# Hybrid block kernel, one core: GpSimd held back at the feed-forward boundaries, squares added on VectorE, and the experts' down projection as three split products

## The chip, the cores and the metric

The kernel runs on one core of a Trainium2 chip. The metric is the device time of one execution in microseconds (us), as the median of several executions. The kernel before took 2161.84 us (median of 3, 2158.42 to 2165.49).

The engines are TensorE (PE in the profile, its weight loads PEld), VectorE (DVE), ScalarE (ACT), GpSimd (POOL) and SyncE (SP), which only issues transfers here. Each runs its own list of instructions in order and waits on semaphores.

## What is computed

Two transformer-like blocks run after each other on 512 tokens of width 1024, in float32. The parts that matter here are the mixture of experts that ends the first block, the two feed-forward layers of the second, and the norms around them. The reference, cut to these:

```python
def hier_moe(h, ...):
    ...
    for gi in range(N_GROUPS):              # 4 groups of 4 experts
        hg = jnp.einsum('td,edf->etf', hf, w_exp_gate[sl])
        hu = jnp.einsum('td,edf->etf', hf, w_exp_up[sl])
        act = jax.nn.silu(hg) * hu * combine[:, sl].T[:, :, None]
        y = y + jnp.einsum('etf,efd->td', act, w_exp_down[sl]).astype(hf.dtype)
...
def swiglu(x, w_in, w_out):
    a, b = jnp.split(x @ w_in, 2, axis=-1)
    return (jax.nn.silu(a) * b) @ w_out
...
    h = h + 0.5 * rms_norm_2(swiglu(rms_norm_2(h, g_ffn1_pre), w_ffn1_in, w_ffn1_out), g_ffn1_post)
    u = rms_norm_2(h, g_mix_pre)
    ...
    h = h + rms_norm_2(mixed, g_mix_post)
    h = h + 0.5 * rms_norm_2(swiglu(rms_norm_2(h, g_ffn2_pre), w_ffn2_in, w_ffn2_out), g_ffn2_post)
```

## The kernel before

**Split products.** Nearly every product is made of three: a float32 operand x is split into hi (x rounded to the fp32r type, a copy on ACT) and lo (x minus hi, a subtraction on DVE or POOL), and PE adds hi*hi, hi*lo and lo*hi in PSUM. In the dense stages ACT makes `w_hi`, POOL makes `w_lo` (`split_chunk`, L722 to L728) from a ring of three weight chunks `w_raw`.

**The experts.** Tokens are sorted by group, so that 7 blocks of 128 rows meet 4 experts each: 28 units (`UNITS`). A unit has three 1 MB chunks of weights: A and B (the two halves of gate and up) and C (down). They lie in 6 slots (`M_SLOTS`), and SP loads a chunk into a slot when PE has used up the chunk six places earlier (semaphore `m_used`), which for A, B and C is two units back. PE's order in its loop over u is: gate_up_half(u+1, A), transpose_act(u), gate_up_half(u+1, B), down(u). ACT copies the hi parts of A and B (L2030, 128x2048 each), DVE subtracts the lo parts (`expert_lo`, L2867). After a unit's gate and up, ACT makes the silu (`silu_of`, L2087), DVE multiplies (`weigh`, L3019, tile `m_act`), PE transposes (L1382) and ACT copies the transposed rows to `m_aT` (`act_rows`, L2093). The down product `down(u)` (L1395) is native float32: 4 matmuls of 512 columns straight from `m_raw` and `m_aT`; the profile shows each as two MATMUL rows. In iteration n ACT's order is hi A(n+2), hi B(n+2), act_rows(n), silu(n+1); DVE's is lo A(n+2), lo B(n+2), weigh(n+1). POOL has nothing in this stage.

**The feed-forward layers.** `swiglu` runs 11 units. A unit has two "seven" chunks (gate, up), computed as seven block products in place of eight (`seven_products`), for which DVE forms sums of weight blocks (`weight_sums`, L2328 to L2332), ACT copies `w_hi` and `wx_hi`, and POOL subtracts `w_lo` (L727) and `wx_lo` (L738, `split_seven`). DVE adds up the seven results (`block_sums`) before PE can use the four PSUM slots again. On entry DVE also splits the normed input by blocks (`h_blocks`, L2300 and L2304). The unit's down product accumulates into `yacc` (L3129).

**The norms.** The sum of squares over the 8 tiles of the feature axis needs all of them: ACT squares each tile (L1647), PE sums the first `own` tiles by products with a column of ones (L905), and DVE adds tiles own+1 to 7 to tile own (`add_square`, L2338), which PE sums last. `SQ_DENSE = 2` is own in the norms next to dense products, `SQ_PACED = 5` in the norm that follows another norm. `keep_clock` (L892) issues products of the identity with itself, whose result nobody reads.

## Time and profile before

| what | value |
|---|---|
| median of 3 runs | 2161.84 us |
| the profiled execution | 2168.82 us, its span 2166.8 us |
| PE busy | 2078.1 us (96%) |
| DVE busy | 1279.4 us (59%) |
| ACT busy | 833.1 us (38%) |
| POOL busy | 788.1 us (36%) |
| moved from HBM | 257.6 MB |
| stages, from the span's start: experts / first feed-forward / second | 654 to 923 / 964 to 1331 / 1797 to 2151 us |

All times in what follows are us from the start of the span. The profile puts a busy PE at 96% of the span; since matmul ends are modelled, this doesn't say that PE computes at its peak for so long. The profiled execution took 7.0 us more than the median of the others.

### The profile page before, as it was taken

The page shows a single profiled execution, that of the slowest core. Times are in us where ns is not written, and L with a number is a line of the kernel's source. Part 1 is how long each engine was busy: PE and PEld are TensorE (multiplying, and loading weights), DVE is VectorE, ACT ScalarE, POOL GpSimd, SP SyncE. Part 2 cuts the span into 40 slices and gives each one's busy share as a digit, 9 for nine tenths or more (in the row PEclk, how much of TensorE's full clock was granted, in tenths as well). Part 3 has the DMA queues.
Part 4 walks back from the last instruction along what each step waited for, and adds up shares of the span by engine and source line. Part 5 has one row for each costly group of instructions (what it writes and reads, how often), then busy time and mean ns, then how long its engine had stood idle before and what let it go on. Part 6 is the DMA issues. An engine that isn't in the chain of part 4 may idle for free.

```text
span 2166.8 us, 31293 instructions
## 1 busy us (share of the span) xinstructions
PE 2078.1 (96%) x12492; PEld 1777.2 (82%) x12492; DVE 1279.4 (59%) x1959; ACT 833.1 (38%) x1018; POOL 788.1 (36%) x595
## 2 busy tenths in 40 slices
PE   4999999999999999979999999999999998999998
PEld 4698787888767666669999999888878788999997
DVE  7375476555465656477677676332431358777775
ACT  7441255222345555344333333343332234333332
POOL 1341233444300000036556552221244435656660
PEclk7898999999989999979999998999999999999999
DMA  9122213555317999712322221111123212223321
GB/s 266 39 79 72 85 59 98 188 191 171 110 59 262 337 342 344 248 59 89 107 97 97 97 97 39 59 59 59 59 78 98 78 59 78 98 97 106 107 97 59
DMA packets 175760, 261.12 MB, mean 121 GB/s; under 512 B 12233, under 2 KB 140922, under 8 KB 175662
## 3 DMA queue, kind: packets, MB, share of 16 engines
q1 hardware_dynamic: 174126, 257.65, 35.8%
q10 hardware_dynamic: 1536, 2.10, 0.3%
q8 instruction: 69, 1.13, 0.2%
q14 instruction: 29, 0.24, 0.0%
HBM read 257.62 MB, written 2.11 MB: 120 GB/s over the span
## 4 chain that ended last, share of the span: by engine, by line
PE 86%; DVE 7%; ACT 4%; issue 1%; POOL 1%; DMA 1%; SPq 0%; DVEq 0%; POOLq 0%; ACTq 0%
PE PS L798 64%; PE PS L1355 7%; PE PS L1395 5%; PE PS L1524 1%; DVE Hf L2368 1%; ACT mod_early L1725 1%; PE PS L892 1%; PE PS L885 1%; DVE Hf L2338 1%; POOL w_lo L727 1%; PE PS L1328 1%; PE PS L1476 1%; DMA mod_early<-in_w_mod 1%; PE PS L905 1%; PE PS L1036 0%
## 5 line engine op out<-in xcount | busy, mean ns | idle before, releaser
L727 POOL TENSOR_TENSOR w_lo<-w_raw,w_hi 128x512 fp32r<-128x512 f32 x444 | 595.5, 1372 | 1287.0 <-ACT w_hi L1703 1265.0
L798 PE MATMUL PS<-HH,w_hi 128*128 128x512 f32 (+2 forms) x1408 | 471.3, 346 | 23.7 <-DVE HL L2291 7.9
L798 PE MATMUL PS<-HL,w_hi 128*128 128x512 f32 (+2 forms) x1408 | 467.3, 343 | 0.0
L798 PE MATMUL PS<-HH,w_lo 128*128 128x512 f32 (+2 forms) x1408 | 465.7, 342 | 0.0
L1703 ACT ACTIVATE w_hi<-w_raw 128x2048 fp32r<-128x2048 f32 x133 | 254.8, 1916 | 392.0 <-DVE w_raw L2329 147.9
L798 PEld LDWEIGHTS PS<-HH,w_hi 128*128 128x128 f32 x1408 | 264.0, 192 | 61.7 <-issue 21.3
L798 PEld LDWEIGHTS PS<-HH,w_lo 128*128 128x128 f32 x1408 | 263.9, 192 | 30.8
L798 PEld LDWEIGHTS PS<-HL,w_hi 128*128 128x128 f32 x1408 | 263.5, 192 | 30.0
L738 POOL TENSOR_TENSOR wx_lo<-wx_raw,wx_hi 128x512 fp32r<-128x512 f32 x132 | 190.0, 1467 | 6.5 <-DVE Hf L2338 6.5
L2867 DVE TENSOR_TENSOR m_lo<-m_raw,m_hi 128x2048 fp32r<-128x2048 f32 x56 | 128.5, 2297 | 76.8 <-ACT m_hi L2030 76.6
L3129 DVE TENSOR_TENSOR yacc<-yacc,PS 128x528 f32<-128x528 f32 (+1 forms) x176 | 117.8, 691 | 49.4 <-PE PS L798 48.6
L798 PE MATMUL PS<-ah,w_hi 128*128 128x264 f32 (+1 forms) x528 | 142.6, 324 | 2.6 <-DVE al L3122 2.6
L2030 ACT ACTIVATE m_hi<-m_raw 128x2048 fp32r<-128x2048 f32 x56 | 107.2, 1916 | 91.9 <-DMA m_raw<-in_w_exp_up 91.9
L798 PE MATMUL PS<-al,w_hi 128*128 128x264 f32 (+1 forms) x528 | 141.5, 322 | 0.0
L798 PE MATMUL PS<-ah,w_lo 128*128 128x264 f32 (+1 forms) x528 | 141.5, 322 | 0.0
L798 PE MATMUL PS<-HHx,wx_hi 128*128 128x264 f32 (+1 forms) x352 | 100.2, 285 | 3.5 <-DVE HLx L2300 2.4
L1395 PE MATMUL PS<-m_raw,m_aT 128*128 128x512 f32 x224 | 101.3, 595 | 1.4 <-ACT m_aT L2093 1.2
L798 PE MATMUL PS<-HHx,wx_lo 128*128 128x264 f32 (+1 forms) x352 | 100.1, 284 | 0.0
L798 PE MATMUL PS<-HLx,wx_hi 128*128 128x264 f32 (+1 forms) x352 | 100.0, 284 | 0.0
L798 PEld LDWEIGHTS PS<-ah,w_hi 128*128 128x128 f32 x528 | 88.5, 190 | 10.5 <-DVE al L3122 3.3
L798 PEld LDWEIGHTS PS<-ah,w_lo 128*128 128x128 f32 x528 | 88.2, 190 | 7.7
L798 PEld LDWEIGHTS PS<-al,w_hi 128*128 128x128 f32 x528 | 88.2, 190 | 7.0
(498 smaller groups left out, 4087.1 us busy)
## 6 DMA issues: line engine op xcount, KB each, us to landing
w_raw<-in_w_in SPq DMA_DIRECT2D x49, 1024.0 KB, 5.1
w_raw<-in_w_ffn_in SPq DMA_DIRECT2D x44, 1024.0 KB, 4.8
m_raw<-in_w_exp_gate SPq DMA_DIRECT2D x56, 512.0 KB, 4.3
m_raw<-in_w_exp_up SPq DMA_DIRECT2D x56, 512.0 KB, 5.4
m_raw<-in_w_exp_down SPq DMA_DIRECT2D x56, 512.0 KB, 4.8
w_raw<-in_w_ffn_out SPq DMA_DIRECT2D x22, 1024.0 KB, 4.8
mod_late<-in_w_mod SPq DMA_DIRECT2D x16, 1024.0 KB, 5.2
mod_early<-in_w_mod SPq DMA_DIRECT2D x8, 1024.0 KB, 11.9
```

The costliest lines, as they stand in the source:

```text
L727: ins = pool.tensor_tensor(w_lo[:, s, cs], w_raw[:, s, cs], w_hi[:, s, cs].bitcast(F32), ALU.subtract)
L738: ins = pool.tensor_tensor(wx_lo[s][:, q], wx_raw[s][:, q], wx_hi[s][:, q].bitcast(F32), ALU.subtract)
L798: ins = mm(o, l, r, **k)
L885: ins = mm(PS[:, s, bank, col:col + G], rsc[0:G, c0 + j:c0 + j + 1].to_broadcast([G, P]), ident[0:G, 0:G], start=True, stop=True)
L892: mm(PS[:, s, 1, 0:P], ident[:, :], ident[:, :], start=True, stop=True)
L905: ins = mm(PS[0:G, s, 0, j:j + 1], Hf[:, k, G * j:G * j + G], ones[:, 0:1], start=k == 0 and j == 0, stop=k == own, skip_group_check=True)
L1355: ins = mm(PS[:, 0, expert_bank(u), :].rearrange("p (g f) -> p g f", g=2), l[:, kk, :], r[:, :, k, :], start=kk == 0 and n == 0, stop=kk = ...
L1395: ins = mm(PS[:, 2 + blk % 2, b, :], m_aT[:, k, :], w[:, k, 512 * b:512 * b + 512], start=ee == 0 and k == 0, stop=ee == N_GRP - 1 and k == 1)
L1703: af(w_hi[:, c % RING, :], w_raw[:, c % RING, :], ACT.Copy).then_inc(hi_done, 1)
L2030: af(m_hi[x][:, :], m_raw[x][:, :], ACT.Copy).then_inc(m_hi_done, 1)
L2867: tt(m_lo[x][:, :], m_raw[x][:, :], m_hi[x][:, :].bitcast(F32), ALU.subtract).then_inc(m_lo_dve, 1)
L3129: W.release(tt(y, y, ps(s, T), ALU.add))
```

## The change

It has four parts.

1. **Down projection.** The transposed activations are split in two (`m_aTH` on ACT, `m_aTL` on DVE), and so is chunk C (`down_hi` on ACT, `down_lo_of` on DVE, 128x2048 each). `down(u)` is 12 products of 512 columns in place of 4 native ones, and waits for `d_lo_done` and `atl_ready`.
2. **Squares.** `SQ_DENSE` becomes 0: in the dense norms DVE adds tiles 1 to 7 to tile 0 and PE sums only that one. The norm before the first feed-forward keeps 2 (`SQ_UNSORT`). PE issues 8 `keep_clock` products before it waits for the sum (`hold`).
3. **POOL.** It waits for the squares' sum before it splits the first chunk of the first feed-forward (before: only between the chunk and its extra blocks), and for the four block sums of the input before the second chunk's extra blocks; and it waits for the sums of the two norms behind the first feed-forward before chunks 1 and 3 of the mixer.
4. **Order.** In `swiglu` the weight sums of the fourth chunk are made before the block sums of the second product and not after them. At the end PE transposes the first half of two tokens' tiles rather than of four before the sum of squares.

```diff
 D = 1024
-SQ_DENSE = 2
+SQ_DENSE = 0
+SQ_UNSORT = 2
 SQ_PACED = 5
...
 m_act = ar("m_act", 33792, [2, P])
-m_aT = ar("m_aT", 34816, [2, P])
+m_aTH = ar("m_aTH", 34816, [2, P], F32R)
+m_aTL = ar("m_aTL", 35840, [2, P], F32R)
 YSH = hf("YSH", KT * TALL * 4, [NTOK, D], F32R)
...
 t_made = sem("expert_act_transposed")
-at_ready = sem("expert_act_rows_ready")
+at_ready = sem("expert_act_rows_hi_ready")
+atl_ready = sem("expert_act_rows_lo_ready")
+d_hi_done = sem("expert_down_hi")
+d_lo_done = sem("expert_down_lo")
 y_added = sem("block_y_added")
...
-    def split_seven(c, s, more=0, sums=None):
+    def split_seven(c, s, more=0, blocks=None):
...
         split_chunk(c, s, more)
-        if sums is not None:
-            pool.wait_ge(sqsum_ready, sums)
+        if blocks is not None:
+            pool.wait_ge(t_ready, blocks)
         pool.wait_ge(hix_done, seven_made(c) + 1 + more * 2)
...
         c = FF_AT[n]
-        split_seven(c, c % RING, sums=2 if n == 0 else None)
+        if n == 0:
+            pool.wait_ge(sqsum_ready, 2)
+        split_seven(c, c % RING)
         if n == 1:
             pool.wait_ge(sqsum_ready, 6)
-        split_seven(c + 1, (c + 1) % RING)
+        split_seven(c + 1, (c + 1) % RING, blocks=4 if n == 0 else None)
         with pool.Fori(0, FF_UNITS - 1) as i:
...
     mixer_at = FF_AT[0] + n_ff
-    rounds = (FF_AT[1] - mixer_at) // RING
+    pool.wait_ge(sqsum_ready, 3)
+    for c in range(mixer_at, mixer_at + RING):
+        if c == mixer_at + 2:
+            pool.wait_ge(sqsum_ready, 4)
+        split_chunk(c, c % RING)
+    rounds = (FF_AT[1] - mixer_at) // RING - 1
     with pool.Fori(0, rounds) as i:
         for s in range(RING):
-            split_chunk(mixer_at + s, (mixer_at + s) % RING, i)
-    for c in range(mixer_at + RING * rounds, FF_AT[1]):
+            split_chunk(mixer_at + RING + s, (mixer_at + s) % RING, i)
+    for c in range(mixer_at + RING * (rounds + 1), FF_AT[1]):
         split_chunk(c, c % RING)
...
-    def sum_squares(T, own):
+    def sum_squares(T, own, hold):
...
             if k == own:
+                keep_clock(hold, s)
                 hcount["sum"] += 1
...
-    def norm(T, own, idle):
-
-        s = sum_squares(T, own)
+    def norm(T, own, hold, idle):
+
+        s = sum_squares(T, own, hold)
         keep_clock(3, s)
...
-    norm(SEQ, SQ_DENSE, 5)
+    norm(SEQ, SQ_DENSE, 8, 5)
...
             pe.wait_ge(at_ready, u - 1)
+            pe.wait_ge(atl_ready, u - 1)
         for k in range(2):
...
         blk, ee = u // N_GRP, u % N_GRP
-        pe.wait_ge(m_landed[x], 32 * (chunk_c(u) // M_SLOTS + 1))
-        pe.wait_ge(at_ready, u + 1)
+        pe.wait_ge(d_lo_done, u + 1)
+        pe.wait_ge(atl_ready, u + 1)
         if ee == 0 and blk >= 2:
             pe.wait_ge(y_added, blk - 1)
-        w = m_raw[x][:, :].rearrange("p (k n) -> p k n", k=2)
+        hi = m_hi[x][:, :].rearrange("p (k n) -> p k n", k=2)
+        lo = m_lo[x][:, :].rearrange("p (k n) -> p k n", k=2)
         for k in range(2):
-            for b in range(2):
-                ins = mm(PS[:, 2 + blk % 2, b, :], m_aT[:, k, :], w[:, k, 512 * b:512 * b + 512],
-                         start=ee == 0 and k == 0, stop=ee == N_GRP - 1 and k == 1)
+            for n, (l, r) in enumerate(((m_aTH, hi), (m_aTH, lo), (m_aTL, hi))):
+                for b in range(2):
+                    ins = mm(PS[:, 2 + blk % 2, b, :], l[:, k, :], r[:, k, 512 * b:512 * b + 512],
+                             start=ee == 0 and k == 0 and n == 0, stop=ee == N_GRP - 1 and k == 1 and n == 2)
         ins.then_inc(m_used, 1)
...
-    norm(TALL, SQ_DENSE, 20)
+    norm(TALL, SQ_UNSORT, 8, 20)
     swiglu(FF_UNITS, TALL)
-    norm(TALL, SQ_DENSE, 28)
-    norm(TALL, SQ_PACED, 20)
+    norm(TALL, SQ_DENSE, 8, 28)
+    norm(TALL, SQ_PACED, 0, 20)
     await_h(now=False)
...
     out_projection()
-    norm(SEQ, SQ_DENSE, 28)
-    norm(SEQ, SQ_PACED, 20)
+    norm(SEQ, SQ_DENSE, 8, 28)
+    norm(SEQ, SQ_PACED, 0, 20)
+
...
     s = W.claim()
-    for k in range(SQ_DENSE):
-        pe.wait_ge(sq_ready, hcount["sq"] + k + 1)
-        for j in range(NTOK):
-            mm(PS[:, s, 0, j:j + 1], Hf[:, k, P * j:P * j + P], ones[:, 0:1], start=k == 0 and j == 0, stop=False,
-               skip_group_check=True)
     pe.wait_ge(gain_diag_ready, 1)
     pe.wait_ge(rtok_ready, 2 * NTOK)
-    for k in range(4):
-        W.wait_released(downs_at + k)
-        for t in range(NTOK):
+    for t in range(2):
+        for k in range(4):
+            W.wait_released(downs_at + k)
             rows_of_y((s + 1 + t) % SLOTS, t, k)
...
     for j in range(NTOK):
-        ins = mm(PS[:, s, 0, j:j + 1], Hf[:, SQ_DENSE, P * j:P * j + P], ones[:, 0:1], start=False, stop=True,
+        ins = mm(PS[:, s, 0, j:j + 1], Hf[:, SQ_DENSE, P * j:P * j + P], ones[:, 0:1], start=j == 0, stop=True,
                  skip_group_check=True)
...
         slot = W.claim()
-        for k in range(4, KT):
+        for k in range(4 if t < 2 else 0, KT):
             if t == 0:
...
             act.wait_ge(m_used, chunk_c(u - 1) + 1)
-        af(m_aT[:, :, :].rearrange("p k n -> p (k n)"), PS[:, 1, u % 2, 0:256], ACT.Copy).then_inc(at_ready, 1)
+        af(m_aTH[:, :, :].rearrange("p k n -> p (k n)"), PS[:, 1, u % 2, 0:256], ACT.Copy).then_inc(at_ready, 1)
+
+    def down_hi(u):
+        x = chunk_c(u) % M_SLOTS
+        act.wait_ge(m_landed[x], 32 * (chunk_c(u) // M_SLOTS + 1))
+        af(m_hi[x][:, :], m_raw[x][:, :], ACT.Copy).then_inc(d_hi_done, 1)
     silu_of(0)
+    down_hi(0)
     block_hi(1)
...
             silu_of(n + 1)
+            down_hi(n + 1)
         if n % N_GRP == 1 and n > N_GRP and n // N_GRP + 1 < BLOCKS:
...
+    def act_rows_lo(u):
+        dve.wait_ge(at_ready, u + 1)
+        tt(m_aTL[:, :, :].rearrange("p k n -> p (k n)"), PS[:, 1, u % 2, 0:256],
+           m_aTH[:, :, :].rearrange("p k n -> p (k n)").bitcast(F32), ALU.subtract).then_inc(atl_ready, 1)
+
+    def down_lo_of(u):
+        x = chunk_c(u) % M_SLOTS
+        dve.wait_ge(d_hi_done, u + 1)
+        tt(m_lo[x][:, :], m_raw[x][:, :], m_hi[x][:, :].bitcast(F32), ALU.subtract).then_inc(d_lo_done, 1)
+
     def add_block(blk):
...
     weigh(0)
+    down_lo_of(0)
     block_lo(1)
...
             expert_lo(2 * n + 5)
+        act_rows_lo(n)
         if n + 1 < UNITS:
             weigh(n + 1)
+            down_lo_of(n + 1)
         if n % N_GRP == 1 and n > N_GRP and n // N_GRP + 1 < BLOCKS:
...
             weight_sums(FF_AT[0] + 1)
-        if m > SQ_DENSE + 1:
-            add_square(Hf, TALL, m - 1, SQ_DENSE)
+        if m > SQ_UNSORT + 1:
+            add_square(Hf, TALL, m - 1, SQ_UNSORT)
     for b in range(1, 5):
...
         weight_sums(at_ + 2)
+        weight_sums(at_ + 3)
         block_sums(actf)
-        weight_sums(at_ + 3)
         gated(0, 0)
...
     real = lambda k: R[:, k, META:TALL]
-    norm(TALL, every, c2(0), SQ_DENSE, split="blocks", while_summed=lambda: clear_y(TALL, 0, 4),
+    norm(TALL, every, c2(0), SQ_UNSORT, split="blocks", while_summed=lambda: clear_y(TALL, 0, 4),
          while_spread=lambda: clear_y(TALL, 4, KT))
...
             weight_sums(FF_AT[1] + 1)
-        if m > SQ_DENSE + 1:
+        if m == 4:
+            for k in range(SQ_DENSE + 1, 4):
+                add_square(Hf, SEQ, k, SQ_DENSE)
+        if m > 4:
             add_square(Hf, SEQ, m - 1, SQ_DENSE)
```

What stands in DVE's list for one unit of the experts in the middle of the stage, before:

```order
L3019 ISA [waits expert_silu_ready]
L3019 SCALAR_TENSOR_TENSOR m_act<-PS,wtab,m_sg 128x128x2
L2867 TENSOR_TENSOR m_lo_222<-m_raw_221,m_hi_223 128x2048 [waits expert_chunk_hi]
L2867 TENSOR_TENSOR m_lo_225<-m_raw_224,m_hi_226 128x2048 [waits expert_chunk_hi]
L3019 ISA [waits expert_silu_ready]
```

and with the change:

```order
L3050 TENSOR_TENSOR m_lo_220<-m_raw_219,m_hi_221 128x2048 [waits expert_down_hi]
L2886 TENSOR_TENSOR m_lo_223<-m_raw_222,m_hi_224 128x2048 [waits expert_chunk_hi]
L2886 TENSOR_TENSOR m_lo_226<-m_raw_225,m_hi_227 128x2048 [waits expert_chunk_hi]
L3044 TENSOR_TENSOR m_aTL<-PS,m_aTH 128x256 [waits expert_act_rows_hi_ready]
L3038 ISA [waits expert_silu_ready]
```

The row of `m_aTL`, for which down(n) waits on PE, stands behind the lo parts of both chunks of unit n+2. ACT's list for the same stretch, before and with the change:

```order
L2030 ACTIVATE m_hi_223<-m_raw_221 128x2048 [waits expert_chunk_landed2]
L2030 ACTIVATE m_hi_226<-m_raw_224 128x2048 [waits expert_chunk_landed3]
L2093 ACTIVATE m_aT<-PS 128x256 [waits expert_chunk_used,expert_act_transposed]
L2087 ACTIVATE m_sg<-PS 128x256 [waits expert_chunk_used,expert_act_ready]
L2030 ACTIVATE m_hi_232<-m_raw_230 128x2048 [waits expert_chunk_landed5]
```

The same stretch of ACT with the change:

```order
L2042 ACTIVATE m_hi_233<-m_raw_231 128x2048 [waits expert_chunk_landed5]
L2042 ACTIVATE m_hi_218<-m_raw_216 128x2048 [waits expert_chunk_landed0]
L2105 ACTIVATE m_aTH<-PS 128x256 [waits expert_chunk_used,expert_act_transposed]
L2099 ACTIVATE m_sg<-PS 128x256 [waits expert_chunk_used,expert_act_ready]
L2110 ACTIVATE m_hi_221<-m_raw_219 128x2048 [waits expert_chunk_landed1]
```

A third copy, that of chunk C, has come in behind each silu. On POOL, at the entry of the first feed-forward, before:

```order
L727 TENSOR_TENSOR w_lo_50<-w_raw_49,w_hi_51 128x512 [waits chunk_hi_done,chunk_extra_blocks_ready]
L727 TENSOR_TENSOR w_lo_50<-w_raw_49,w_hi_51 128x512 x3
L738 TENSOR_TENSOR wx_lo0_180<-wx_raw0_179,wx_hi0_181 128x512 [waits chunk_extra_hi_done,squares_of_last_tiles_added]
...
L727 TENSOR_TENSOR w_lo_50<-w_raw_49,w_hi_51 128x512 [waits chunk_hi_done,chunk_extra_blocks_ready]
...
L738 TENSOR_TENSOR wx_lo1_183<-wx_raw1_182,wx_hi1_184 128x512 [waits chunk_extra_hi_done]
```

and with the change:

```order
L732 TENSOR_TENSOR w_lo_50<-w_raw_49,w_hi_51 128x512 [waits chunk_hi_done,chunk_extra_blocks_ready,squares_of_last_tiles_added]
L732 TENSOR_TENSOR w_lo_50<-w_raw_49,w_hi_51 128x512 x3
L743 TENSOR_TENSOR wx_lo0_180<-wx_raw0_179,wx_hi0_181 128x512 [waits chunk_extra_hi_done]
...
L732 TENSOR_TENSOR w_lo_50<-w_raw_49,w_hi_51 128x512 [waits chunk_hi_done,chunk_extra_blocks_ready]
...
L743 TENSOR_TENSOR wx_lo1_183<-wx_raw1_182,wx_hi1_184 128x512 [waits chunk_extra_hi_done,h_block_sums_ready]
```

The wait for the squares has moved ahead of the first chunk, and the second chunk's extra blocks have a new one.

## Rows read from the trace of the kernel before

**Rows 1.** Windows of 40 us: busy time and (count) by engine, PE clock, DMA share, GB/s.

```profile
760.00:800.00 40.00, 40.00 (x152) 27.33 (x151) 23.88 (x15) 20.92 (x18) 0.00 (x0) 1.00 0.96 341
```

**Rows 2.** Instructions by line, 700 to 880: count, busy us, mean ns, idle before and releaser.

```profile
L2867 DVE TENSOR_TENSOR m_lo<-m_raw,m_hi 128x2048 fp32r<-128x2048 f32 x39 | 89.4, 2293 | 57.3 <-ACT m_hi L2030 57.3
L2030 ACT ACTIVATE m_hi<-m_raw 128x2048 fp32r<-128x2048 f32 x38 | 72.9, 1917 | 65.7 <-DMA m_raw<-in_w_exp_up 65.7
```

**Rows 3.** Chain of waits, 640 to 960: start, us, engine and line.

```profile
673.07 3.43 PE PS L1395 x8
...
839.67 3.43 PE PS L1395 x8
846.08 2.77 PE PS L1355 x12
848.85 3.43 PE PS L1395 x8
```

**Rows 4.** Timeline of SP, 820 to 860: start, us, line, operation.

```profile
839.84 0.33 SPq L648 DMA_DIRECT2D m_raw<-in_w_exp_gate  x1
```

**Rows 5.** Timeline of ACT, 820 to 850, the same columns, idle before in brackets.

```profile
846.14 1.92 ACT L2030 ACTIVATE m_hi<-m_raw 128x2048 fp32r<-128x2048 f32 x1 [1.68 <-DMA m_raw<-in_w_exp_up]
847.96 0.36 ACT L2093 ACTIVATE m_aT<-PS 128x256 f32<-128x256 f32 x1
```

**Rows 6.** Timeline of DVE, 820 to 850.

```profile
848.09 2.29 DVE L2867 TENSOR_TENSOR m_lo<-m_raw,m_hi 128x2048 fp32r<-128x2048 f32 x1 [1.31 <-ACT m_hi L2030]
```

**Rows 7.** Timeline of ACT at the first units of the experts.

```profile
668.16 3.71 ACT L2030 ACTIVATE m_hi<-m_raw 128x2048 fp32r<-128x2048 f32 x2
```

**Rows 8.** Timeline of DVE before the first feed-forward.

```profile
935.53 0.69 DVE L2329 TENSOR_TENSOR w_raw<-w_raw 128x512 f32<-128x512 f32 x1
...
938.91 1.27 DVE L2328 TENSOR_TENSOR wx_raw<-w_raw 128x512 f32<-128x512 f32 x1
940.10 1.79 DVE L2329 TENSOR_TENSOR w_raw<-w_raw 128x512 f32<-128x512 f32 x1
941.92 1.67 DVE L2331 TENSOR_TENSOR wx_raw<-w_raw 128x512 f32<-128x512 f32 x1
943.63 1.64 DVE L2332 TENSOR_TENSOR wx_raw<-w_raw,wx_raw 128x512 f32<-128x512 f32 x1
```

**Rows 9.** Timeline of POOL, the same stretch.

```profile
938.32 6.40 POOL L727 TENSOR_TENSOR w_lo<-w_raw,w_hi 128x512 fp32r<-128x512 f32 x4 [323.66 <-ACT w_hi L1703]
```

**Rows 10.** Timeline of DVE in the first feed-forward's first unit.

```profile
987.78 0.43 DVE L3090 TENSOR_TENSOR actf<-fp,PS 128x264 f32<-128x264 f32 x1 [4.66 <-ACT fp L2130]
```

**Rows 11.** Chain of waits, entry of the first feed-forward.

```profile
1002.07 58.00 PE PS L798 x461
```

**Rows 12.** Timeline of DVE at the end of the first feed-forward.

```profile
1314.39 2.87 DVE L3122 TENSOR_TENSOR al<-actf,ah 128x528 fp32r<-128x528 f32 x2
...
1330.35 1.06 DVE L2338 TENSOR_TENSOR Hf<-Hf 128x528 f32<-128x528 f32 x1
```

**Rows 13.** Chain of waits, the same stretch.

```profile
1317.32 9.11 PE PS L798 x60
```

**Rows 14.** Windows of 4 us there, columns as in Rows 1.

```profile
1316.00:1320.00 4.00, 2.68 (x12) 2.68 (x13) 2.50 (x3) 0.00 (x0) 3.64 (x3) 0.66 0.23 42
```

**Rows 15.** Chain of waits, entry of the second feed-forward.

```profile
1834.32 5.79 POOL wx_lo L738 x3
```

**Rows 16.** Chain of waits, the last 90 us.

```profile
2135.47 1.22 DVE al L3122 x2
...
2151.71 1.68 PE PS L1591 x16
2153.39 3.68 PE PS L1582 x32
...
2158.99 2.73 DVE o_tok L3328 x4
```

**Rows 17.** Timeline of ACT, the last 70 us.

```profile
2151.75 0.60 ACT L2266 ACTIVATE R_tok<-PS 128x512 f32<-128x512 f32 x1 [0.72 <-PE PS L1576]
```

## The prediction

> **What bounds the kernel now.** I read the windows of 40 us first, then the groups by line in the experts' stage, then the chain of waits, then the timelines around the places that the chain names. In the middle of the experts PE is on record as busy all the time and the transfers take 0.96 of the DMA engines' time; DVE has 23.9 of 40 us, ACT 20.9, POOL nothing [rows 1]. The chain there stays on PE: a down product takes 3.43 us for 4 native matmuls, a half of gate and up 2.77 us for 12 split ones, and from one down to the next there are 9.18 us [rows 3]. Two things stand close to it. The DMA queue would carry the stage by itself in 0.96 x 9.18 = 8.8 us a unit. And ACT waits for chunks before its copies (65.7 us in 38 waits) and DVE for ACT (57.3 in 39) [rows 2]: each chunk reaches them only just after they have nothing else to do. Outside this stage I looked at the two entries and the two ends of the feed-forward layers, where the chain leaves PE.
>
> **The experts, step by step.** *PE.* 12 split matmuls cost 2.77 us [rows 3] where the native ones cost 3.43: PE's own work falls from 9.18 to 8.5 us a unit. *ACT and DVE.* A unit adds a copy of 1.92 us and a subtraction of 2.29 us (the same shapes as in [rows 2]), and `m_aTL`, a subtraction of 256 columns out of PSUM, for which the nearest row is 0.43 us [rows 10]. DVE goes from 5.5 to 8.2 us a unit, ACT from 4.8 to 6.7: neither is over 9.
>
> *The order is what costs.* `m_aTL` of unit n stands in DVE's list behind the lo parts of A and B of unit n+2, and down(n) on PE waits for it. Chunk B(n+2) can't be asked for before PE has used B(n). In the unit at 848.85: PE ends B(n) as the down product at 839.67 starts [rows 3], SP issues at 839.84 [rows 4], ACT starts its copy at 846.14, on landing [rows 5], 6.30 us later; the copy takes 1.92, and DVE's subtraction runs from 848.09 to 850.38 [rows 6]. Now down(n) needs only `m_aT`, which ACT has at 848.32 [rows 5], half a us before PE comes to it at 848.85. With the change it needs 850.38 + 0.43 + about 0.1 = 850.9, 2.05 us after PE came free even at today's pace. So down(n) starts 11.2 us after the end of B(n) at the earliest. B(n+1) ends 8.5 us of PE work after down(n-1) starts, and down(n+1) comes 11.2 us behind that: two units in 8.5 + 11.2 = 19.7 us, 9.85 a unit. The landing of 6.30 us includes a queue that a slower pace thins out. The other end is a landing of 5.3 us, a guess of one us less: (8.5 + 10.2) / 2 = 9.35. I take 9.7, nearer the row, since C, A and B are still asked for about 3 us apart. That is 0.5 us over 9.18, in 26 of the 28 units: +13 us (+4.5 to +17).
>
> *The first unit.* ACT's copies of A(2) and B(2) run from 668.16 to 671.87 [rows 7], and the first down starts at 673.07 [rows 3]. Now a copy of C and a subtraction come ahead of them: ACT ends B(2) 1.9 us later, at about 674, and DVE, which first takes C (2.3 us, from about 669.2), casts a block and clears a tile (some 1.6 us) and then has two subtractions of 2.3, at about 677.7; with `m_aTL` the first down starts near 678.3, 5 us late. The last two units have no later chunks in front of `m_aTL`, but PE waits for `m_aTL` itself: I count them at nothing. Experts together **+18 us** (+9 to +24).
>
> **Squares and POOL before the first feed-forward.** While POOL splits the first chunk for 6.40 us [rows 9], DVE's second set of weight sums takes 1.27 + 1.79 + 1.67 + 1.64 = 6.37 us, where the same subtraction costs 0.69 with POOL idle [rows 8], 2.76 for four. These lie on the way to the sum of squares, on which PE waits. With POOL held until that sum they cost 3.6 us less. What POOL puts off (its 6.40 us and the extra blocks) fits into the some 13 us between the sum and PE's first product, so nothing comes late for it. The held second chunk spares `h_blocks` some 0.5 us more. A rule of the Trainium skill (SBUF — State Buffer, Who interferes with whom) says that a DVE instruction with two inputs in SBUF and a GpSimd instruction that reads SBUF exclude each other, and that the later one blocks for the whole length of the other. By that rule each of the four could wait out one of POOL's pieces, 6.40 / 4 = 1.6 us, and the gain of the hold could be 6.4 us. The rows show 3.6 us, less than the rule allows, and I take the rows.
>
> **Order of the weight sums.** The fourth chunk's sums come ahead of the second product's block sums. They now run where POOL splits the third chunk, so I take the 6.4 us of [rows 8] for them. Today the block sums start at 987.78 [rows 10], which with the 3.6 us from above would be 984.2. The fourth chunk lands at about 981 (my estimate: it is asked for when PE begins the second chunk), and 6.4 us later it is 987.4: the block sums are 3 us late, and PE, which needs a PSUM slot from them, waits some 2.5 us. In return the fourth chunk, for which PE waits until 1002.07 [rows 11], is ready earlier. Shift of 3.6 us included, I get between -3 and -5.5 us for the first layer, **-3.9**. In the second there is no shift: the chain passes POOL's extra blocks at 1834.32, 5.79 us [rows 15]; they start earlier, PE's third chunk later: **-0.6** (+1.5 to -2.5).
>
> **End of the first feed-forward.** PE waits for `al`, which takes 2.87 us while POOL splits a mixer chunk [rows 12], against 1.22 to 1.28 undisturbed [rows 16]: -1.5 us. PE then starts at 1317.32 [rows 13] after a gap of 2 us, and the granted clock is 0.66 in the window 1316 to 1320 [rows 14], a drop to 1.2 GHz for part of it, worth 1.6 us; with the gap at 0.5 us I expect none. The adds of squares take 1.06 [rows 12] instead of 0.7: -0.5. Together **-3.6** (-2 to -4). The two more adds of a dense norm fall into the pauses between PE's products and add nothing; the sums that PE no longer makes, and the 8 products of the identity, lie in its wait for the sum.
>
> **The last us.** PE's sums of two tiles (1.68 us) go, and 16 of the 32 first transposes (3.68 us) move behind the sum [rows 16]. But PE then waits for ACT's last copy, 2151.75 + 0.60 [rows 17], and for token tiles 3 and 4 it has 16 transposes each against DVE's 1.36 us (2.73 for two, [rows 16]): **-1.9** (-1.2 to -2.7).
>
> **The sum.** 18 - 3.9 - 0.6 - 3.6 - 1.9 = +8.0 us. The profiled execution took 2168.82 us for a span of 2166.8; it would take 2176.8. It lies 7.0 us over the median of the runs, and I forecast from the median: 2161.84 + 8 = **2169.8 us**.
>
> **The rivals.** *The landing shortens* (0.27): at the lower ends, 9.35 us a unit, the experts cost +9 and the rest gives 10: 2161. For it: the queue is at 0.96 only because three chunks are asked for in 9.18 us. Against: chunks still come in threes, 3 us apart.
> *PE sets the pace* (0.13): if `m_aTL` were in time, PE's 0.66 us a unit would be gained until the queue's 8.8 us bind, -0.38 x 27 = -10, with the rest -10: 2142. For it: PE is on the chain now, with no wait. Against: the 2.05 us of [rows 6].
> *PE's waits bring its clock down* (0.15), the slower end: the waits of 1 to 2 us in each unit are as long as the gap before 1317.32, which was followed by 0.66 of the clock [rows 13, 14]. Each such drop costs 1.6 us; it decides from about four of them on. With one in every third unit +14 more: 2184. The Trainium skill (TensorE: Matmul & The Clock Gate, A second HAM failure mode) has PE's clock swing when it idles briefly but often between groups of matmuls. By that rule every unit could pay the 1.6 us: +43, 2213. No row here shows such a stage, and I leave that end out of the range.
> *POOL's holding back gives nothing* (in the same 0.15), if what it puts off comes late: only the experts' +18 remains, 2180.
>
> **How the numbers follow.** My forecast has 0.45. About 0.3% (6.5 us) is what a measurement of this kernel can tell from no change, so slower begins at 2168.3: two thirds of the forecast's cases and all of the clock's, 0.46; same takes the rest and nearly all of the short landings, 0.41; faster 0.13. The range for 8 in 10 goes from 2154 to 2182: it leaves out the case in which PE sets the pace and half of the clock's.
>
> **What would show it.** In the changed profile: (1) downs 9.7 us apart, not 9.2 or 8.8, DMA share near 0.91, and PE waiting for DVE's `m_aTL`, about 1.2 us a unit; (2) the first down at about 678; (3) four weight sums before the first feed-forward at 0.69 us each, and the gap between the last unsorted tile and the sum 3.6 us shorter; (4) a PE wait of 2 to 3 us before the third chunk of both layers; (5) `al` at 1.3 us before the last down of the first layer, and the clock at 1.00 there. If (1) shows downs 9.2 apart or less, the step on the order in DVE's list is wrong, and with it the sign.

## The result and the profile after

The changed kernel is slower. Its median is 2195.89 us (2193.11 to 2203.75, 4 runs), beside 2163.66 us (2158.42 to 2167.56) for the kernel before in the same session: a ratio of 1.0144, 95% interval 1.0124 to 1.0164, or +31 us. I had forecast +8 and a range up to 2182. The sign was right and the size was not.

The profiled execution has a span of 2191.4 us, 24.6 more than that of before. By stages, from the end points that both traces have:

| stage | before, us | after, us | difference |
|---|---|---|---|
| start to first gate and up product | 654.3 | 652.6 | -1.7 |
| from there to the first down | 18.6 | 24.0 | +5.4 |
| first down to the 25th | 221.7 | 246.9 | +25.2 |
| to the end of the last block's add | 28.6 | 30.6 | +2.0 |
| to the sum of squares before the first feed-forward | 27.9 | 23.2 | -4.7 |
| to the scaling by that norm | 6.0 | 4.6 | -1.4 |
| first feed-forward, to the sum of squares behind it | 376.6 | 379.4 | +2.8 |
| its two norms | 23.7 | 25.1 | +1.5 |
| mixer and its two norms | 432.8 | 430.9 | -1.9 |
| second feed-forward, to its sum of squares | 363.5 | 362.6 | -0.9 |
| the rest | 13.1 | 11.5 | -1.6 |

The experts lose 32.6 us, everything behind them gains 6.2 (the rest is the start). In the middle of the experts, the row of the windows that answers to [rows 1] (columns: busy us and instructions of PE, PE's loads, DVE, ACT, POOL; then the granted clock, the DMA share and GB/s):

```profile
760.00:800.00 40.00, 34.48 (x152) 27.61 (x152) 32.51 (x22) 26.41 (x22) 0.00 (x0) 1.00 0.89 319
```

PE is idle for 5.5 of 40 us, in which nothing was idle before, and DVE and ACT have the work that was added. The chain of waits shows where, in place of [rows 3] (start, length, what):

```profile
698.42 3.04 PE PS L1411 x12
701.46 2.80 PE PS L1368 x12
704.26 0.22 PE PS L1396 x2
704.48 2.77 PE PS L1368 x12
...
707.40 0.33 SPq L653
...
707.82 6.55 DMA m_raw<-in_w_exp_up
...
714.40 1.92 ACT m_hi L2042
...
716.35 0.60 DVE m_lo L2886
716.95 1.61 issue
718.56 0.43 DVE m_aTL L3044
718.98 0.14 issue
719.12 3.04 PE PS L1411 x12
```

This is the loop that the prediction described: PE ends chunk B at 707.25, its slot is loaded anew, ACT copies (from 714.40, 7.00 us after SP's issue, near the top of the 5.6 to 7.2 us that the twelve late chunks take), DVE subtracts (716.35 to 718.56, split in two pieces here), and only then comes `m_aTL`, for which the down product waits. Between the two downs shown stands one more, at 707.07, that waits for nothing: a down waits in every second unit only. From 698.42 to 719.12 are 20.7 us for two units, where before two took 18.4.

The second set of weight sums before the first feed-forward, DVE's timeline, beside [rows 8]:

```profile
968.55 0.69 DVE L2347 TENSOR_TENSOR wx_raw<-w_raw 128x512 f32<-128x512 f32 x1
...
970.60 0.69 DVE L2351 TENSOR_TENSOR wx_raw<-w_raw,wx_raw 128x512 f32<-128x512 f32 x1
```

All four are undisturbed (those left out take 0.69 too). What POOL put off disturbs DVE later instead, in the entry of the feed-forward (POOL's timeline, then DVE's; these three cost 3.58 us together before):

```profile
998.88 6.74 POOL L743 TENSOR_TENSOR wx_lo<-wx_raw,wx_hi 128x512 fp32r<-128x512 f32 x3 [5.87 <-DVE HXr L2323]
998.72 5.76 DVE L2319 TENSOR_TENSOR HLx<-HXr,HHx 128x1056 fp32r<-128x1056 f32 x3
```

The end of the first feed-forward, chain of waits, beside [rows 12, 13]:

```profile
1343.22 1.25 DVE al L3154 x2
...
1344.51 0.41 PE PS L810
...
1344.93 4.90 DMA w_raw<-in_w_in
...
1349.86 1.91 ACT w_hi L1715
1351.77 1.08 ACT Hf L1659 x2
...
1352.87 0.72 DVE Hf L2357
...
1361.32 0.71 PE PS L918 x7
```

`al` takes 1.3 us and the last down product, from 1344.51, 12.07 us in place of 13.49, at a granted clock of 1.00 (1344.5 to 1356): as forecast. But the chain no longer runs over PE. ACT stands at a copy of the next mixer chunk until that lands, makes the squares only behind it, and DVE works off seven adds of squares among its adds of products until 1361.28. From the start of the last down product to the sum it takes 16.8 us, where before it took 16.4.

At the very end, two rows beside [rows 16, 17]:

```profile
2177.92 0.61 ACT R_tok L2285
...
2178.78 2.02 PE PS L1599 x16
```

PE waits for ACT's last copy, as forecast, and the last us are 1.6 shorter.

### The profile page after: what moved, and what is told of

It is laid out like the page before. It is cut to its first block, busy times and chain, and to the rows that moved or that the text cites. A ratio compares the mean times of both kernels' runs of the same rounds, so it can differ in the third digit from the quotient of the medians.

```text
span 2191.4 us, 31595 instructions
## 1 busy us (share of the span) xinstructions
PE 2064.2 (94%) x12596; PEld 1797.1 (82%) x12596; DVE 1365.6 (62%) x2023; ACT 884.2 (40%) x1046; POOL 789.3 (36%) x595
## 4 chain that ended last, share of the span: by engine, by line
PE 83%; DVE 7%; ACT 4%; DMA 3%; issue 3%; SPq 0%; DVEq 0%; ACTq 0%
PE PS L810 63%; PE PS L1368 5%; PE PS L1411 3%; DMA m_raw<-in_w_exp_up 2%; PE PS L1540 1%; PE PS L904 1%; ACT mod_early L1737 1%; PE PS L918 1%; PE PS L1341 1%; DVE Hf L2387 1%; DVE Hf L2357 1%; ACT m_hi L2042 1%; DMA mod_early<-in_w_mod 1%; PE PS L1492 1%; DVE HL L2319 1%
## 5 line engine op out<-in xcount | busy, mean ns | idle before, releaser
L2886 DVE TENSOR_TENSOR m_lo<-m_raw,m_hi 128x2048 fp32r<-128x2048 f32 x56 | 127.3, 2284 | 16.6 <-ACT m_hi L2042 15.8
L2145 ACT ACTIVATE ah<-actf 128x1056 fp32r<-128x1056 f32 (+1 forms) x22 | 23.7, 1076 | 145.3 <-DVE actf L3147 145.3
```

What stands on the lines that cost most here:

```text
L2145: af(ah[:, par, :, 0:T], actf[:, :, 0:T], ACT.Copy).then_inc(ah_ready, 1)
L2886: tt(m_lo[x][:, :], m_raw[x][:, :], m_hi[x][:, :].bitcast(F32), ALU.subtract).then_inc(m_lo_dve, 1)
```

## The experiments

All ratios are to the kernel before, measured in the same session; the changed kernel's is 1.0144. Differences in us between kernels are differences of these ratios times 2163.66.

**The two halves apart.** The changed kernel with native downs (`down`, `act_rows` and the lists of ACT and DVE around them as before), and the kernel before with split downs alone.

```diff
-for n, (l, r) in enumerate(((m_aTH, hi), (m_aTH, lo), (m_aTL, hi))):
-    for b in range(2):
-        ins = mm(PS[:, 2 + blk % 2, b, :], l[:, k, :], r[:, k, 512 * b:512 * b + 512], ...)
+for b in range(2):
+    ins = mm(PS[:, 2 + blk % 2, b, :], m_aT[:, k, :], w[:, k, 512 * b:512 * b + 512], ...)
```

> The change without its second half: the down projection is again 4 native matmuls, everything else (squares, POOL's holds, order of weight sums, last us) stays as in the changed kernel. Theory (the terms outside the experts are worth what the two traces show, about -8 us in the profiled spans): 2156 us, 5 to 9 us under the kernel before; downs again 9.2 us apart, first down near 671.3, four weight sums ahead of the first feed-forward at 0.69 us each, last down of the first feed-forward to the sum of squares no shorter than before (16.4 us). Rival (those parts only shift waits and give nothing once the experts are quick): 2162 to 2165 us, the same as the kernel before.

> The kernel before with the split down projection alone. Theory (the two halves of the change add up and the experts cost 32.6 us, as between the two traces): 2193 to 2199 us, downs 10.3 us apart in the mean, in pairs of 20.5 to 20.8 us, first down near 678. Rival (part of the loss in the changed kernel comes from the higher clock and the shifted start that the other half brings): under 2188 us.

Measured: 0.9964 (0.9951 to 0.9977), -7.8 us, and 1.0188 (1.0170 to 1.0206), +40.7. The parts outside the experts are worth what the theory said (e1); the last down of the first feed-forward to its sum is indeed no shorter. The split downs cost more than either of my figures. In sum the halves make 32.9 us, against 31.2 for both together: they add up. My figures for the second came from the 32.6 us between two profiled executions, and the profiled one of the changed kernel was the quickest of its four. In e2 7 of the 14 downs that wait take 4.4 to 5.5 us, in the first profile of the changed kernel 5 do. That made the clock a suspect.

**The place of `m_aTL`.** Nothing is added or left out; only the lists of ACT and DVE change.

```diff
     if n + 2 < UNITS:
         expert_hi(chunk_a(n + 2))
+    act_rows(n)
+    if n + 2 < UNITS:
         expert_hi(chunk_b(n + 2))
-    act_rows(n)
...
     if n + 2 < UNITS:
         expert_lo(2 * n + 4)
+    act_rows_lo(n)
+    if n + 2 < UNITS:
         expert_lo(2 * n + 5)
-    act_rows_lo(n)
```

> The changed kernel, but m_aTH and m_aTL of unit n are made between chunk A and chunk B of unit n+2, on ACT and on DVE; no work is added or left out. Theory (all of the loss is the place of m_aTL behind the late chunk B): m_aTL is ready 6.9 us after the end of B(n) on PE, before PE ends B(n+1) at 8.8 us, so PE or the DMA queue sets the pace: 8.8 to 9.0 us a unit without pauses, clock at 1.00, DMA share 0.96 to 0.99, and about 32 to 37 us less than the changed kernel: 2156 to 2164 us. Rival 1 (the added work on ACT and DVE is what costs, since DVE has 8.2 us of work a unit and chunks come late to PE): PE then waits for m_lo in place of m_aTL, units over 9.8 us, 2185 us or more. Rival 2 (the clock falls because of the splits' denser use of PE): downs of 4.5 us and a granted clock below 0.97 in the stage, 2170 to 2180 us.

Measured: 0.9933 (0.9918 to 0.9948), 46 us under the changed kernel and 14.5 under the one before. From the first to the 25th down 214.2 us, 8.92 a unit. The window:

```profile
740.00:780.00 40.00, 38.10 (x169) 30.11 (x167) 36.40 (x26) 30.14 (x25) 0.00 (x0) 1.00 0.98 348
```

DVE has 36.4 of 40 us of work, more than in the changed kernel, and it doesn't matter: rival 1 falls. The DMA engines are at 0.98 and the clock stays at 1.00, so rival 2 falls too. The experts' loss was the order, not the work.

**A later `m_aTL`.** It is computed three times in a row.

```diff
-tt(m_aTL, PS, m_aTH, ALU.subtract).then_inc(atl_ready, 1)
+for again in range(3):
+    ins = tt(m_aTL, PS, m_aTH, ALU.subtract)
+    if again < 2:
+        L(ins)
+ins.then_inc(atl_ready, 1)
```

> The changed kernel, with the subtraction that makes m_aTL done three times in a row, each after the one before (the same values), so that m_aTL comes about 1.1 us later in each unit. Theory (the wait sits in every second unit only: one down is late, the next follows on PE without a wait): a pair of units grows by 1.1 us, 0.55 a unit, +14 to +16 us: 2210 to 2213 us. Rival (each unit waits for its own m_aTL): +1.1 us a unit, +28 to +31 us: 2224 to 2228 us. Third case (m_aTL is not on the path and the pace is the landing of chunks alone): within 4 us of the changed kernel.

Measured: 1.0240 (1.0200 to 1.0280), 21 us over the changed kernel: between the theory's 14 to 16 and the rival's 28 to 31, so the time alone decides nothing. The chain does:

```profile
747.07 0.43 DVE m_aTL L3045
...
747.53 0.43 DVE m_aTL L3045
...
748.10 5.46 PE PS L1411 x12
753.56 2.88 PE PS L1368 x12
```

Still it is every second down that waits long (three of the others wait 0.3 to 0.8 us), but it then takes 5.46 us, not 3.04: behind a wait of 4.1 us the granted clock from 748.1 to 753.5 is 0.50, which is 1.2 GHz in place of 2.4, where the down at 719.12 in the changed kernel has 1.00. 8 of the downs take 5.3 to 5.5 us and 3 more 4.3 to 4.6, and the granted clock in the windows of 40 us is 0.83 to 0.90 from 700 to 860 us (0.96 and 1.00 in the two behind). So there are two prices, the wait and a lower clock behind it.

**The waits filled.** To take the clock's price away without touching the wait, PE gets products of the identity in front of the downs that wait, 10 of them in the changed kernel, 14 in the one with the later `m_aTL`.

```diff
+if u % 2 == 0 and u < UNITS - 2:
+    for _ in range(10):
+        mm(PS[:, 1, (u + 1) % 2, 256:384], ident[:, :], ident[:, :], start=True, stop=True)
 down(u)
```

> The changed kernel, with 10 products of the identity (some 2 us of work whose result nobody reads) on PE ahead of the down product of every second unit, the ones that wait; they lie inside the wait for m_aTL. Theory (the lower clock after a wait is a price of its own on top of the wait): no down product takes 4.4 to 5.5 us any more, all take 3.0, the waits' ends stay where they were, and 5 to 8 us come off the changed kernel, 2191 to 2194 us where it had 2199. Rival (the long down products have another cause, such as PSUM or DVE): long ones stay, and the time stays or grows by up to 5 us.

> The kernel with m_aTL made three times (e4), with 14 products of the identity on PE ahead of the down product of every second unit. There 10 of 14 of the downs that wait took 5.3 to 5.5 us. Theory (the waits themselves cost about 15 us over the changed kernel, the rest is the clock, about 2.4 us after each long wait): 15 to 24 us off it, 2201 to 2210 us, no long downs. Rival (each unit pays for its late m_aTL, the clock costs nothing): 2222 to 2228 us.

Measured: 1.0071 (1.0058 to 1.0085), 15.8 us under the changed kernel, and 1.0147 (1.0132 to 1.0163), 20 us under e4. In both only the last down, which I hadn't filled, is long. Window and chain of the first:

```profile
780.00:820.00 40.00, 38.94 (x193) 32.11 (x192) 32.39 (x23) 26.19 (x21) 0.00 (x0) 1.00 0.89 313
```

```profile
787.90 2.77 PE PS L1368 x12
790.67 2.23 PE PS L1423 x20
792.90 0.98 issue
793.88 3.04 PE PS L1411 x12
```

The wait ends where it did, `m_aTL` is no earlier, and the down takes 3.04. With the clock out of the way the later `m_aTL` costs what the theory says: from the first down to the 25th 253.5 us against 243.5, 10.0 us for 12 pairs of units, 0.83 a pair for two subtractions of 0.43. But filling gave twice the 5 to 8 us that I had read from one profile.

**The changed kernel again**, unaltered, for a second profile.

> The changed kernel once more, unaltered, for a second profile and more times. Filling PE's waits (e5) took some 16 us off the median of the changed kernel, while in its first profiled execution, the shortest of its four, the long down products sum to only about 7 us. Theory (the number of waits after which the clock falls differs between executions, and the first profile had few): this profile shows 7 or more long down products with 10 us or more in sum, where its span is longer, and the median is 1.3 to 1.6% over the kernel before. Rival (the first profile is typical and the filling gains in another way): 5 long ones again, 7 us, at a span of 2195 us or more.

Measured: 1.0144 (1.0114 to 1.0173), the same ratio. The profiled execution has a span of 2201.3 us and 11 long downs of the 14 that wait, where the first had 5. One window, and the chain within it:

```profile
820.00:860.00 40.00, 34.84 (x136) 27.47 (x136) 32.25 (x22) 24.10 (x20) 0.00 (x0) 0.87 0.80 282
```

```profile
827.33 0.43 DVE m_aTL L3044
...
827.89 5.46 PE PS L1411 x12
833.35 3.13 PE PS L1368 x12
```

From the first down to the 25th it takes 260.3 us, 13.4 more than in the first profile. Take from both what the long downs have over 3.04 us (16.3 and 4.5) and 244.0 and 242.4 remain, beside 243.5 for the filled kernel. So the wait costs 21 to 22 us over the 221.7 of before in each; the clock adds from 4.5 to 16 in this stretch, by the execution. The wait ahead doesn't tell which: in the first profile a wait of 2.33 us at 820.04 was followed by 4.51 us, one of 2.25 at 840.99 by 3.04, and in the second one of 3.25 at 893.69 by 3.04.

**Is the landing a queue?** From the third unit on the load of chunk C brings an eighth of its bytes; ACT and DVE keep the size of their work.

```diff
+n = D if c < 3 * 2 + 4 else D // 8
-sp.dma_start(m_raw[x][:, D * k:D * k + D], ...)
+sp.dma_start(m_raw[x][:, D * k:D * k + n], ...)
```

> The changed kernel, but from the third unit on the load of chunk C (down weights) brings only an eighth of its bytes; ACT's copy reads those repeatedly and DVE's subtraction takes m_hi from itself, so that their work keeps its size; the down products are then not those of the reference. Theory (landing of chunk B, 6.6 to 7.0 us from issue, is one of 3 us for its own bytes plus a queue behind A and C, because loads are issued in bursts 2.5 to 3 us apart however slow the mean pace is): B lands in 5 us or less, a pair of units takes 18.7 to 19.3 us, and 18 to 27 us come off the changed kernel: 2172 to 2181 us. Rival (the time from issue to landing is fixed and has no queue in it): landing 6.3 to 7 us, time within 5 us of the changed kernel.

Measured: 1.0116 (1.0101 to 1.0132), 6 us off, not 18 to 27. SP's, ACT's and DVE's timelines around one late chunk B:

```profile
783.60 0.33 SPq L653 DMA_DIRECT2D m_raw<-in_w_exp_gate  x1
...
789.30 1.92 ACT L2043 ACTIVATE m_hi<-m_raw 128x2048 fp32r<-128x2048 f32 x1 [1.32 <-DMA m_raw<-in_w_exp_up]
...
789.21 4.50 DVE L2892 TENSOR_TENSOR m_lo<-m_raw,m_hi 128x2048 fp32r<-128x2048 f32 x2
793.62 0.42 DVE L3050 TENSOR_TENSOR m_aTL<-PS,m_aTH 128x256 fp32r<-128x256 f32 x1
```

From issue to copy there are 5.7 us. Over all twelve late chunks the mean is 5.9 us, against 6.5 in the changed kernel (6.6 in its second profile): so part of the landing is a queue, but seven eighths of chunk C's bytes are worth only 0.65 us of it, where the theory had put 1.6 or more. From ACT's copy to `m_aTL` it takes 4.2 us here as there, so DVE's list adds next to nothing (under 0.1 us in the mean, although in the place shown it is behind by an add of a block). A pair of units without a long down accordingly takes 19.6 us where it took 20.2 to 20.3. 9 of the 14 downs that wait are long, with the clock's price behind each. The theory's direction held, its size didn't. The down products of this kernel are not the reference's, and its interval just overlaps that of the changed kernel (1.0124 to 1.0164), so the landings carry the argument and not the 6 us.

**The squares at the end of the first feed-forward.** On top of the early rows of e3, ACT's copy of the next mixer chunk moves behind the squares.

```diff
         next_hi()
         W.skip(KT)
-    next_hi()
     W.skip(KT)
...
-norm(TALL, lambda k: yacc[:, k, 0:TALL], split=False)
+norm(TALL, lambda k: yacc[:, k, 0:TALL], split=False, ahead=1)
```

> e3 (rows made before chunk B), and in addition ACT makes the squares at the end of the first feed-forward before its copy of the next mixer chunk, for whose landing it otherwise waits. Theory (the two further adds of squares were late only because ACT stood behind that landing, so DVE had a backlog up to the sum): last down product's start to the sum of squares 14.2 to 14.8 us where the changed kernel has 16.8, and 2 to 2.5 us under e3: about 2152 us on a chip where e3 has 2154.7. Rival (DVE's seven adds of 0.7 us among seven adds of a product are a chain of their own and end no earlier): 16.3 us or more, no change.

Measured: 0.9898 (0.9883 to 0.9913), 7.6 us under e3 and 22 under the kernel before, the quickest here. From the start of the last down product to the sum 14.4 us, as expected; but 2 to 2.5 us was not all. The chains of both from the sum on, e7 first:

```profile
1317.36 1.10 PE PS L918 x12
1318.46 0.78 PE PS L904 x6
1319.24 1.65 PE PS L897 x12
```

```profile
1324.82 1.92 PE PS L918 x12
1326.73 1.49 PE PS L904 x6
1328.22 2.49 PE PS L897 x12
```

The same small instructions take 3.5 us against 5.9: the granted clock over them is 0.91 in the one and 0.50 in the other. In e7 the sum comes 2.3 us after the down product's end, in e3 5.0; after the 8 products of the identity that fill the start of this wait PE is idle for 0.6 us in e7 and 3.3 in e3. It is no chance of one execution: in all five profiles with the squares ahead of the copy (e7 and e9 to e12) these instructions take 3.3 to 3.6 us, in seven of the changed kernel and its variants with the copy first 4.6 to 5.9. In the two profiles 2.7 us are gained up to the sum and 3.8 in the two norms behind it.

**Each of POOL's holds, and the order of the weight sums, undone on e7.**

> e7 with POOL's two holds before the first feed-forward undone (POOL again splits the first chunk while DVE adds squares and weight sums, and its second chunk follows at once). Theory (the hold is worth the second set of weight sums, 0.7 us each in place of 6.4 for four, less what POOL then disturbs later, h_blocks and HLx): end of the last block's add to the sum of squares 27 to 28 us in place of 23; from that sum to the last down product 1.5 to 2.5 us shorter; net +2 to +4 us, a ratio to the kernel before of 0.991 to 0.992 where e7 has 0.9898. Rival (what is put off costs as much at the entry as it saved): 0.9895 to 0.9900.

> e7 with the order of the weight sums as in the kernel before (the fourth chunk's after the second product's block sums), in both feed-forwards. Theory A (the first entry came out 2.4 us longer than before because POOL, held back, now shares the port with h_blocks; the order itself is worth -0.3 there and -0.6 in the second, as forecast): 0 to 2 us slower than e7, ratio 0.990 to 0.991, third-chunk products start 1 to 2 us earlier and fourth-chunk ones wait again. Theory B (the order costs those 2.4 us in the first): 1 to 3 us faster than e7, ratio 0.9885 to 0.9893.

> e7 with POOL's holds on the first four mixer chunks undone (it splits them as soon as they land, beside the end of the first feed-forward and its two norms). Theory (as in the prediction: al takes 2.9 us in place of 1.3, PE's gap before the last down product is 2 us and its clock falls there, adds of squares take 1.06): +2.5 to +4 us, ratio 0.991 to 0.992, last down product 13 us or more. Rival (that gap is covered by DVE's adds of squares anyway): under 1 us, ratio 0.9895 to 0.9902.

Measured: 0.9924 (0.9907 to 0.9941), 0.9911 (0.9895 to 0.9928) and 0.9930 (0.9912 to 0.9948), beside 0.9898 (0.9883 to 0.9913) for e7. The intervals touch or overlap, so the places in the traces have to carry it, and they carry only a part: the medians lie 5.6, 2.8 and 6.9 us over e7's, the stages below explain 1.4, 1.3 and 1.6, and where the rest lies isn't shown. Without the first hold the four weight sums are slow again (DVE's timeline of e9):

```profile
932.68 1.26 DVE L2345 TENSOR_TENSOR wx_raw<-w_raw 128x512 f32<-128x512 f32 x1
...
937.39 1.64 DVE L2349 TENSOR_TENSOR wx_raw<-w_raw,wx_raw 128x512 f32<-128x512 f32 x1
```

The sum is 3.5 us later there (27.9 us after the last block's add, against 24.4), and the first feed-forward 2.1 us shorter (373.8 against 375.9): the hold moves POOL's disturbance, and keeps a part of the gain. With the old order of weight sums the first feed-forward is 1.3 us longer (377.2), so theory B, by which the new order costs time, falls; A is not shown by the times. Without the mixer's holds, the chain of e11:

```profile
1304.28 2.80 DVE al L3150 x2
...
1307.13 12.12 PE PS L805 x96
```

`al` is slow again and the feed-forward 1.6 us longer, but in this execution the clock did not fall behind the gap of 2 us, against my expectation of 13 us or more for that product.

**A last fill**, 7 products of the identity ahead of the first and of the last down of e7.

> e7 with 7 products of the identity ahead of the first and of the last down product, where PE waits 1.7 and 2.1 us for m_aTL. Theory (the wait before the last one brings the clock down in most executions, 4.4 us in place of 3.0; the first one is not followed by a fall): 0 to 2 us under e7, ratio 0.989 to 0.990, last down product 3.0 us. Rival (the fill makes PE late): 0.5 to 2 us over e7.

Measured: 0.9913 (0.9892 to 0.9933), not to be told from e7. In e7's own profile the last down took 3.00 us behind its wait of 2.07, so there was nothing to gain in that execution.

## Why the prediction was wrong in size

**The mechanism was right.** `m_aTL` behind the late chunk B is the whole loss (e3), it strikes every second unit (e4 and e6), and the first down comes 5.4 us late, 5 forecast.

**The step "I take 9.7" failed, and below it two terms.** Without the clock a pair of units takes 20.2 to 20.3 us, I had 19.4. The first term is the landing: the step's own working gave 19.7 a pair, and I went under it because "a slower pace thins out" the queue in the landing. It didn't: from SP's issue to ACT's copy the late chunks B take 5.6 to 7.2 us, 6.5 in the mean, where chunks B took 6.2 in the mean before (5.4 to 7.3; the row in [rows 4, 5] had 6.30). The pace is slower only in the mean. SP issues chunks at 701.49, 704.43, 707.40, 710.02, 712.89 and 715.88, one every 2.9 us, where before they came every 3.1, and then none for 6.3. The line of the DMA engines' busy tenths for 700 to 880 us, in 40 slices, of after and then of before:

```profile
DMA  4999579996899879995999779992999879992999
```

```profile
DMA  9998999999989999999999999999999999999998
```

The idle time lies in one hole per pair of units, and the late chunk is never asked for in a hole. e8 shows that there is a queue to shorten, so the rival "the landing shortens" failed on its reason, not on its premise. The other term is PE's part of the pair, which is 8.8 us and not 8.5: a split down behind a wait takes 3.04 us, for which I had the 2.77 of gate and up with the same 12 products. So of the 0.8 us a pair that I lacked 0.3 are the discount on the landing, 0.2 its growth and 0.3 PE's part. Over the 24 units between the first and the 25th down I had +12 us, and +21 to +22 were measured without the clock.

**The clock was a rival and should have been a term.** I gave the lower clock 0.15, as a case apart, at one drop of 1.6 us in every third unit. It came on top of the slower pace, since the pace is what makes the waits: 5 drops in the first profile, 11 in the second, each worth 1.5 us, or 2.4 where the whole down ran slowly. Filling the waits took 15.8 us off the median. The Trainium skill (TensorE: Matmul & The Clock Gate, A second HAM failure mode) has the clock swing where PE idles briefly but often between groups of matmuls; the trace agrees that it does, in 5 to 11 of the 28 units. I had read it as one drop in every unit, +43 us, and left that end out; what the clock took was 8 to 20 us an execution.

The experts' sum in the first profile is then 5.4 (first unit) + 20.7 (pace) - 1.8 (the last units, without the clock) + 8.3 (clock) = 32.6, against 18. For the median e1 gives 39, from 31.2 + 7.8: that leaves some 15 us for the clock, and filling took 15.8.

**Behind the experts** the sum was -10 and e1 measured -7.8 (-5 to -10.6). That the two lie so close is in part luck: the stages show two terms that came out wrong by 2.5 us and more (below), and -1.4 before the first scaling and -1.9 in the mixer, for which the forecast had no term. Point (3), the weight sums: 0.69 each, and the stretch to the sum 4.7 us shorter, 3.6 forecast; undoing the hold gives 3.5 back. (The 1.6 us for one piece of POOL's work in the prediction contained a wait of POOL itself: the shortest such piece takes 1.26, and DVE lost some 1.0 us to each.) "Nothing comes late for it" was wrong: up to `al` the first feed-forward is 3.9 us longer than before, where -0.3 was forecast for it. 2.1 of them are the hold, by e9 against e7; about 1.1 are the clock.

Point (4): PE waits 1.8 us before the third chunk of the first feed-forward and 3.0 in the second, about as said, but I had not counted what follows: the granted clock is 0.68 over the next 5.4 us in both. In e7, behind the same wait in the first (1.8 us), it is 1.00, and PE is 1.1 us further on. Some 0.7 us stay open.

Point (5): `al` at 1.3 us and no drop of the clock, right; but "the two more adds of a dense norm fall into the pauses between PE's products" failed, because the squares that they add come from ACT, and ACT was waiting for a landing. Of the 3.6 us 1.1 were left (1.5 on `al` and 1.4 on the last down product, less 1.8 behind it), and e7 shows what was there: 6.5 us in the profiles against e3, with the clock of the norms behind it, and 7.6 in the medians. The last us: -1.6 for -1.9.

## What to carry to other kernels

A small operation for which the critical engine waits must not be queued behind one that waits for the latest transfer: look for it in the list of every engine that it passes, and move it ahead before judging the change by its work (here the same work, ordered otherwise, went from +1.4% to -0.7%). When a change makes PE wait a few us again and again, count its clock as a term on top of the waits, and take it from more than one profiled execution. And a slower mean pace shortens no queue if the idle time gathers in one hole: look at the spacing of the issues.

## What the runs showed of the hardware that I had not expected

- The same kernel has a lower granted clock after 5 of its 14 waits in one execution and after 11 in another, at the same lengths of wait (2.1 to 3.9 us). All 10 waits of 3.8 us or more in these two, e2 and e4 were followed by a long down.
- With some 2 us of products of the identity within each wait of about 3 us the granted clock stayed at 1.00 in all windows of 40 us from 700 to 900 us, and no filled down was long.
- The drop is felt in short work too: the small instructions of a norm took 4.6 to 5.9 us where the sum came 5 us after the last product (PE idle for the last 3 of them) and 3.3 to 3.6 where it came 2.3 us after it (idle for 0.6).
